# Moved small loads, an undrained block end and a last pair by column halves in an encoder layer

## The reference

```python
h = x + token_mixer(rms_norm(x, g_attn_norm), w_in, ..., w_out)
y = h + hier_moe(rms_norm(h, g_ffn_norm), ...)

def token_mixer(a, ...):
    c_q, c_kv, k_r, u = split(a @ w_in)            # 384, 256, 64, 512 columns
    q = (rms_norm(c_q) @ w_uq)                     # 4 heads of 192, RMS-norm per head, rotary on 64
    kv = (rms_norm(c_kv) @ w_ukv)                  # 4 heads of 128 + 128
    attn = softmax(q k^T / sqrt(192)) v            # both directions
    return concat([attn, multi_scale_pool(u)]) @ w_out

def hier_moe(x, ...):                              # 4 groups of 8 experts, top group, top 2 in it
    for e in range(32):
        hdn = silu(x @ w_gate[e]) * (x @ w_up[e])  # 1024 -> 256
        y = y + combine[:, e:e + 1] * (hdn @ w_down[e])
```

## Time and profile before

| | us |
|---|---|
| median of 3 runs (647.74 to 649.58) | 649.23 |
| the profiled execution | 643.12 |
| its span, first to last instruction | 641.5 |
| TensorE busy | 537.6 (84%) |
| VectorE busy | 216.9 (34%) |
| ScalarE busy | 168.7 (26%) |
| GpSimd busy | 137.8 (21%) |
| DMA | 140.69 MB, mean 219 GB/s |

### The profile page before, as it was taken

One profiled execution on the slowest core, in us unless ns is written; L12 is line 12 of the kernel. 1 busy time (PEld: TensorE's weight loads), 2 busy tenths in 40 slices (PEclk: granted clock), 3 DMA queues, 4 the chain that ended last, 5 costly groups with the idle time before them and its releaser, 6 DMA issues.

```text
span 641.5 us, 9145 instructions
## 1 busy us (share of the span) xinstructions
PE 537.6 (84%) x3140; PEld 380.6 (59%) x3141; DVE 216.9 (34%) x646; ACT 168.7 (26%) x412; POOL 137.8 (21%) x214
## 2 busy tenths in 40 slices
PE   3979999999898889899962989999878995778861
PEld 2859888887344477788852546665546653444540
DVE  2663342351768662445573111121111111111110
ACT  3563434332464521222331201121111111111100
POOL 6022321321154100011114002321201321101110
PEclk9989999999899999999985989999999999988887
DMA  8920000000432009433359979999999999999961
GB/s 202 379 104 22 13 34 1 0 1 1 170 100 65 1 33 372 180 130 112 100 188 370 351 230 393 382 370 379 381 368 415 393 382 360 375 379 389 395 233 20
DMA packets 28589, 140.69 MB, mean 219 GB/s; under 512 B 6339, under 2 KB 7078, under 8 KB 16246
## 3 DMA queue, kind: packets, MB, share of 16 engines
q1 hardware_dynamic: 20496, 122.89, 49.1%
q0 software_dynamic: 6288, 14.04, 9.2%
q10 hardware_dynamic: 1766, 3.25, 1.7%
HBM read 131.15 MB, written 16.46 MB: 230 GB/s over the span
## 4 chain that ended last, share of the span: by engine, by line
DMA 44%; PE 42%; DVE 6%; SPq 2%; issue 2%; ACT 2%; POOL 1%; POOLq 0%
DMA expert_w<-in_w_down 20%; DMA expert_w<-in_w_up 18%; PE ps L450 8%; PE ps L451 7%; PE ps L455 7%; DMA w_uq_raw<-in_w_uq 3%; PE ps L615 3%; PE ps L556 3%; PE ps L779 2%; PE ps L570 2%; DMA x_res<-in_x_prompt 2%; DMA g_rows<-token_rows,idx_all 1%; PE ps L795 1%; PE ps L573 1%; SPq L369 1%
## 5 line engine op out<-in xcount | busy, mean ns | idle before, releaser
L779 PE MATMUL ps<-expert_w,xT 128*64 128x256 f32 x1152 | 131.2, 384 | 19.7 <-DMA expert_w<-in_w_up 8.3
L779 PEld LDWEIGHTS ps<-expert_w,xT 128*64 128x64 f32 x1152 | 96.8, 138 | 58.0 <-issue 29.4
L795 PE MATMUL ps<-expert_w,hT 128*64 128x512 f32 x288 | 73.9, 659 | 18.7 <-DMA expert_w<-in_w_down 13.2
L1544 POOL DMA_INDIRECT out<-y_sb,idx_now x18 | 28.7, 1596 | 190.2 <-issue 142.2
L1387 DVE SCALAR_TENSOR_TENSOR hid<-s_act,gate,ps 128x256 f32<-128x256 f32 x18 | 12.0, 667 | 144.4 <-ACT s_act L1025 144.4
L795 PEld LDWEIGHTS ps<-expert_w,hT 128*64 128x64 f32 x288 | 24.9, 150 | 56.1 <-issue 56.1
L1025 ACT ACTIVATE s_act<-ps,gate 128x256 f32<-128x256 f32 x18 | 8.5, 473 | 134.3 <-PE ps L779 134.3
L450 PE MATMUL ps<-w_in_hi,aT_hi 128*128 128x384 f32 (+2 forms) x120 | 43.7, 369 | 0.0
L1399 DVE COPY y_sb<-ps 128x512 f32<-128x512 f32 x18 | 12.4, 692 | 86.3 <-PE ps L795 86.3
L451 PE MATMUL ps<-w_in_lo,aT_hi 128*128 128x384 f32 (+2 forms) x120 | 40.9, 345 | 0.0
L1030 ACT ACTIVATE y_sb<-ps 128x512 f32<-128x512 f32 x18 | 10.7, 597 | 89.6 <-PE ps L795 89.6
(11 more groups left out here) (235 smaller groups left out, 927.7 us busy)
## 6 DMA issues: line engine op xcount, KB each, us to landing
expert_w<-in_w_gate SPq DMA_DIRECT2D x32, 1024.0 KB, 9.5
expert_w<-in_w_up SPq DMA_DIRECT2D x32, 1024.0 KB, 9.1
expert_w<-in_w_down SPq DMA_DIRECT2D x32, 1024.0 KB, 9.8
w_in_raw<-in_w_in SPq DMA_DIRECT2D x8, 608.0 KB, 19.3
w_out_raw<-in_w_out SPq DMA_DIRECT2D x8, 512.0 KB, 3.8
out<-h_sb SPq DMA_DIRECT2D x6, 512.0 KB, 4.6
token_rows<-h_sb ACTq DMA_DIRECT2D x6, 512.0 KB, 4.9
x_sb<-in_x_prompt SPq DMA_DIRECT2D x4, 512.0 KB, 10.5
```

The lines of the kernel that those rows point to most:

```text
L779: mm = pe.matmul(ps[r, 2, g * FH:(g + 1) * FH], xT[:, q.o, k, r], w_gu(b, lane, k, g), start=(k == 0), stop=(k == KD - 1))
L795: mm = pe.matmul(ps[r, 4 + half, :], hT[:, q.o, k, r], w_dn(b, lane, k, half), start=(k == 0), stop=(k == 1))
L1544: pool.indirect_dma_start(out=out, out_offset=bass.IndirectOffsetOnAxis(ap=idx, axis=0), in_=y_sb[:, buf, :], in_offset=None, compute_op=A ...
```

## The change

Three edits in one.

1. The 14 DMAs at the head of GpSimd's list are issued by SP. The rotary table and the six broadcast gains stand behind w_ukv, ahead of the third x tile; the token numbers, routers, FFN gains, slot table and zeros (`small_tables`) stand behind the fourth x tile. VectorE multiplies the router's weights in token tile 4 instead of tile 1.
2. The block is opened with `no_gpsimd_drain=True`.
3. In the last pair w_down is loaded as four DMAs, column half by column half (`load_last_down`; the first two wait for `part_in[1]`, the others for `part_in[2]`, as the two of before did), TensorE waits for each half's load and signals after each half (`down_halves`), ScalarE copies the left half after the first signal, VectorE the right half after the second, and GpSimd adds each half by itself (`add_half`), with `out` seen as 1,536 rows of 512 columns and indices `idx_last` = 2 x token + half, which four small VectorE operations make ahead of the first pair. The second add doesn't wait for the first.

```diff
-        block = ctx.enter_context(nc.Block())
+        block = ctx.enter_context(nc.Block(no_gpsimd_drain=True))
...
             sp.dma_start(w_ukv[:, :, :], a["w_ukv"][0].rearrange("(k p) n -> p k n", k=KKV)).then_inc(w_ukv_in, 16)
+            small = [(rope_tab[:, :, :, :].rearrange("p n t r -> p (n t r)"), a["rope"])]
+            half = DR // 2
+            for n, name in enumerate(("g_q_head", "g_k_head")):
+                g = a[name][0:1, DN:DQK]
+                small += [(g_rope[:, 2 * n, :], g.partition_broadcast(P)),
+                          (g_rope[:, 2 * n + 1, 0:half], g[:, half:DR].partition_broadcast(P)),
+                          (g_rope[:, 2 * n + 1, half:DR], g[:, 0:half].partition_broadcast(P))]
+            with nc.allow_non_contiguous_dma(reason="a few hundred short rows"):
+                for dst, src in small:
+                    sp.dma_start(dst, src).then_inc(gains_in, 16)
...
                 load_x(i)
+                if i == 3:
+                    small_tables()
...
+            def load_last_down(j, b):
+                src = a["w_down"][0].rearrange("(l j) (p k) (n f) -> j n p l k f", l=2, k=2, n=2)
+                for n in range(2):
+                    sp.wait_ge(part_in[1 + n], 16 * (j + 1))
+                    for lane in range(2):
+                        dst = weights[b][:, lane, 2, :].rearrange("p (k n f) -> p n k f", k=2, n=2)
+                        sp.dma_start(dst[:, n], src[j, n, :, lane]).then_inc(part_in[4 + n], 16)
...
+            def down_halves(b, n):
+                pe.wait_ge(main.hT_done, n + 1)
+                for half in range(2):
+                    pe.wait_ge(part_in[4 + half], 16 * (n + 2))
+                    for k in range(2):
+                        for lane in range(2):
+                            r = slice(lane * LANE, (lane + 1) * LANE)
+                            mm = pe.matmul(ps[r, 4 + half, :], hT[:, 0, k, r], w_dn(b, lane, k, half),
+                                           start=(k == 0), stop=(k == 1))
+                    mm.then_inc(main.y_mm, 1)
...
-                if i == 1:
+                if i == 4:
                     dve.wait_ge(router_in, 16 * N_ROUTER)
...
+            for lane in range(2):
+                r = slice(lane * LANE, (lane + 1) * LANE)
+                last_slots = ps[r, 5, PAIRS * (lane + 1) - 1:PAIRS * (lane + 1)]
+                for n in range(2):
+                    dve.tensor_scalar(idx_last[r, n:n + 1], last_slots, 2.0, 2.0 * NO_TOKEN + n, ALU.mult, ALU.add).then_inc(idx_done, 1)
...
+            def add_half(n, buf):
+                c = slice(n * 512, (n + 1) * 512)
+                pool.indirect_dma_start(out=out.rearrange("t (n f) -> (t n) f", n=2),
+                                        out_offset=bass.IndirectOffsetOnAxis(ap=idx_last[:, n:n + 1], axis=0),
+                                        in_=y_sb[:, buf, c], in_offset=None, compute_op=ALU.add,
+                                        bounds_check=2 * T - 1, oob_is_err=False).then_inc(main.added, 16)
...
+                if last:
+                    ready((idx_done, 13), (main.y_act, j + 1), (main.added, 16 * j))
+                    add_half(0, b)
+                    ready((main.y_dve, j + 1))
+                    add_half(1, b)
...
-            pool.wait_ge(main.added, 16 * PAIRS)
+            pool.wait_ge(main.added, 16 * (PAIRS + 1))
```

More of the change, by code:

```diff
@@ L364, in load_x, with small_tables @@
                 sp.dma_start(x_sb[:, i % 2, :], x_dram(i)).then_inc(x_in[i % 2], 16)
+            def small_tables():
+                with nc.allow_non_contiguous_dma(reason="short rows"):
+                    for dst, src in ((tok_ids[:, :], a["tokens"]),
+                                     (w_router[:, :, 0:EG], a["w_group_router"][0].rearrange("(k p) n -> p k n", k=KD)),
+                                     (w_router[:, :, EG:], a["w_expert_router"][0].rearrange("(k p) n -> p k n", k=KD)),
+                                     (g_router[:, :], a["g_ffn_norm"][0].rearrange("(k p) -> p k", k=KD)),
+                                     (g_x[:, :], a["g_ffn_norm"][0].rearrange("(p k) -> p k", k=KD))):
+                        sp.dma_start(dst, src).then_inc(router_in, 16)
+                sp.dma_start(slot_table.rearrange("(a b) c -> a (b c)", a=P),
+                               a["slots"].rearrange("(a b) c -> a (b c)", a=P)).then_inc(setup_dram, 16)
+                sp.dma_start(out[T:T + P, :], a["zeros"]).then_inc(setup_dram, 16)
             load_x(0)
@@ L425, in refill @@
                 used(lambda q: q.y_mm)
-                load_pair(sp, j, b, range(4, 6))
+                if isinstance(j, int):
+                    load_last_down(j, b)
+                else:
+                    load_pair(sp, j, b, range(4, 6))
             with sp.Fori(1, PAIRS // 3) as i:
@@ L807, in pair @@
                 hidden_transposes(main, j)
-                for n in range(4, 6):
-                    pe.wait_ge(part_in[n], 16 * (j + 1))
-                pe_y_free(pe, j)
-                down(main, b, j)
+                if last:
+                    pe_y_free(pe, j)
+                    down_halves(b, j)
+                else:
+                    for n in range(4, 6):
+                        pe.wait_ge(part_in[n], 16 * (j + 1))
+                    pe_y_free(pe, j)
+                    down(main, b, j)
                 def again(n, p):
@@ L1394, in hT_copy, with y_copy @@
                 dve.tensor_copy(hT[:, q.o, :, :], ps[:, 3, 0:FH].rearrange("p (k t) -> p k t", k=2)).then_inc(q.hT_done, 1)
-            def y_copy(q, n, buf):
-                dve.wait_ge(q.y_mm, n + 1)
+            def y_copy(q, n, buf, last=False):
+                dve.wait_ge(q.y_mm, n + 2 if last else n + 1)
                 y_free(dve, q, n)
@@ L1409, in pair @@
                 hT_copy(main, j)
-                y_copy(main, j, b)
+                y_copy(main, j, b, last)
                 def again(n, p):
@@ L1573, in more_add @@
             def more_add(j, n):
-                ready((over.y_act, n + 1), (over.y_dve, n + 1), (main.added, 16 * (j + 1)))
+                halves = 1 if isinstance(j, int) and j == PAIRS - 1 else 0
+                ready((over.y_act, n + 1), (over.y_dve, n + 1), (main.added, 16 * (j + 1 + halves)))
                 add_rows(over, n, 3, idx_now[:, 6:7])
@@ L1588, in pair @@
                     gather_pair(j + 2, (b + 2) % 3, 2 * j + 1)
-                set_idx(3 + b, j)
-                waits = [(idx_set, add_count(j)), (main.y_act, j + 1), (main.y_dve, j + 1)]
-                if not (isinstance(j, int) and j == 0):
-                    waits.append((main.added, 16 * j))
-                ready(*waits)
-                add_rows(main, j, b, idx_now[:, 3 + b:4 + b])
+                if not last:
+                    set_idx(3 + b, j)
+                if last:
+                    ready((idx_done, 13), (main.y_act, j + 1), (main.added, 16 * j))
+                    add_half(0, b)
+                    ready((main.y_dve, j + 1))
+                    add_half(1, b)
+                else:
+                    waits = [(idx_set, add_count(j)), (main.y_act, j + 1), (main.y_dve, j + 1)]
+                    if not (isinstance(j, int) and j == 0):
+                        waits.append((main.added, 16 * j))
+                    ready(*waits)
+                    add_rows(main, j, b, idx_now[:, 3 + b:4 + b])
                 todo = pool.value_load(counts_i[0:1, 3, bass.ds(j, 1)], min_val=0, max_val=PASSES - 1)
```

30 lines of the change are left out of this document (5 added, 25 removed).

## The result

| | before | after |
|---|---|---|
| executions, us | 649.23, 649.58, 647.74, 649.05 | 624.22, 624.80, 629.76, 624.97 |
| median, us | 649.14 | 624.88 |
| profiled execution, us (its span) | 643.12 (641.5) | 624.22 (622.6) |

The ratio is 0.9646, 95% interval 0.9595 to 0.9697: the changed kernel takes 19.7 to 26.3 us less, 24.3 us by the medians. From the one profiled execution to the other it is 18.9 us, and there the forecast was 19.2.

A forecast was written before the change was run, and what follows sets the result against it. Bound: w_uq's late load for the first 35 us, then mostly TensorE to 340 us, expert weights from 377. Head 10.4 (9.1 + 1.3), drain 5.2 and tail 3.6 sum to 19.2 us off 649.23: 630.0, range 627 to 637.

The forecast's parts named there:

- the last step: Sum at the end: 10.4 + 5.2 + 3.6 = 19.2 us, subtracted from the timed median 649.23, gives 630.0.
- the tail: Last pair by column halves: matmuls start at hT's end, last landing at 631.9 against 635.5; 3.6 us, between 1.8 and 5.5.
- the head by w_uq: Start of the kernel: w_uq lands earlier, line 873 starts between 25.2 and 26.1 instead of 34.9; 9.1 us gained.
- the clock in tile 0: First token tile: TensorE hardly stands, so eight matmuls escape the low clock; 1.3 us, or 0.
- the drain: Closing barrier: GpSimd's 5.22 us drain goes with nothing beside it, so 5.2 us count in full.
- the issuer alone: Small loads: if the part changed only the issuer, it would give nothing by the skill's rule; time 640.4.
- Rope tables: Line 1122: table and six broadcasts land at 28 us at 15 ns a short row, 33 us being free.
- rival (b): Head held by something else, rope tables at the q0 price or slow early w_in rows: about 4 us remain, 636.4; chance 0.10.
- Other small loads: Seven loads behind the fourth x tile: 5 us, delaying at most the fifth tile, which has 28.7 us of slack.
- Rival (d): Short rows clog SP's in-order queue, the fifth x tile is late, slower than before: 651; chance 0.03.
- Rival (a): End of program: the drain's time comes back behind the block, profiled time minus span growing to 7 us: 635.2; chance 0.16.
- Rival (c): Last pair: halves give nothing, two short-row adds taking as long as one and weights landing late: 633.6; chance 0.08.

The follow-up runs named there:

- a2_after_look: The changed kernel, not altered, profiled a second time: 620.74 us.
- g1: The changed kernel with the 14 small loads issued by GpSimd, but late (seven once w_ukv has landed, seven in token tile 2): 629.12 us, ratio 0.9709.
- h1: The kernel before with only the small loads moved to SP behind the weights; drain and last pair as before: 635.11 us, ratio 0.9798.
- s1: The changed kernel with all 14 small loads issued by SP ahead of the weights, right behind the constants: 637.48 us, ratio 0.982.
- b1: An exact copy of the kernel before, timed and profiled again: 649.94 us, ratio 1.001.
- b2: An exact copy of the kernel before, run for another profile: 646.0 us.
- b4: An exact copy of the kernel before, run for another profile: 645.46 us.
- b3: An exact copy of the kernel before, run for another profile: 647.93 us.
- d1: The kernel before with only the GpSimd drain at the end of the block removed: 643.5 us, ratio 0.9915.
- t1: The kernel before with only the last pair's down loads, matmuls, copies and row-adds done by halves: 641.24 us, ratio 0.9888.
- n1: The changed kernel with the small loads back on GpSimd at the start; no drain and the last pair by halves stay: 639.67 us, ratio 0.9869.

## Why the prediction was right and wrong

**The step that failed** is the size of the gain that the last step took off the median: "The median of the timed runs is 649.23, 6.1 above the profiled one; I subtract from the median: 630.0". What was taken off was 10.4 + 5.2 + 3.6 = 19.2 us; the stages show 22.7 in the mean and the medians 24.3. Every term was short: the tail 3.6 against 5.1, the head by w_uq 9.1 against 10.1, the clock in tile 0 1.3 against 2.0, the drain 5.2 against 5.5. They were read from one execution that had a short head, a short attention and a short tail, and taken off the median of executions in which most of these were longer; and the range was built only from the bounds of the prices. A gain read in a short head and a short tail is too small for the usual ones. Of the 5.1 us between 630.0 and 624.88, 1.7 are terms that were short even from profile to profile, 1.8 more are the difference between that profile and the mean, and 1.6 no run places.

The 18.9 measured between the two profiled executions against 19.2 looks like a hit, and so does 624.22 against 623.9, and it is partly chance: the attention of the changed kernel's profiled execution was a long one, which hid 2.2 us of the gain. Had I written that the two executions may differ by 2 to 3 us in stages that the change doesn't touch, the range would have reached down by that much, to the result.

**Term by term**, with the means of the stage table (eight profiles with the old head, seven with the old tail; five with the new head, a2_after_look among them, four of these for the tile loop, since g1's late tables lengthen it; five with the new tail; the end of h1, whose drain was short, left out):

| term | predicted | profile to profile | mean of stages |
|---|---|---|---|
| w_uq, line 873 | 9.1 (8.8 to 9.7) | 9.4 | 10.1 |
| clock in tile 0 | 1.3 (0 to 1.3) | 1.4 | 2.0 |
| no drain | 5.2 (5.2 to 5.3) | 5.6 | 5.5 |
| tail | 3.6 (1.8 to 5.5) | 4.5 | 5.1 |
| sum | 19.2 | 20.9 | 22.7 |

Profile to profile the other stages take back 2.0 us of the 20.9. Of the 24.3 us between the medians the means explain 22.7; the rest is less than the interval's half width of 3.3. Each term lies above the middle that I took, three of them above the end that I had for them, none by more than 0.7 us. The misses have one sign, in part because three of them share a source, the short head, low stretch and tail of the profile of before; but from profile to profile the tail is already 0.9 short and the head 0.3. The end's 0.3 to 0.4 us is the handshake of the barrier behind the drain, which shrank too (before: 635.5 to 641.5 with 5.22 of drain; after: 622.2 to 622.6).

**Head: right, mechanism and place.** q0 is gone, the rows come 1.5 us apart, w_uq is scaled at 25.5 (forecast: before 26.2), line 873 starts at 25.41 (25.2 to 26.1). I took the later of two landings, 23.5; it was 22.88. TensorE and ScalarE end together, at 25.1 and 25.5, as worked out. That it is the order and not the issuer is shown in the head by the two runs on it (40.0 and 26.75 us), as the prediction had it. What I priced there, 640.4 for the issuer alone, came out as 637.5, but not by nothing changing: its head is 3.2 us longer than the mean before, its tile loop 2.0 shorter, and the rest of the difference is open.

**Clock in tile 0: right, and larger.** In a stretch of 5 us from about the first c transposes on the eight profiles with the old head show a granted clock of 0.50 to 0.78, behind a stand of 2.4 to 3.1 us, the changed kernel 1.00 behind one of 0.98, and s1, where TensorE stands 1.07 us ahead of them, loses nothing either. The profile that I read had a short low stretch, 3.4 us; it and the three others with one (b1, b2, b4) have a tile loop of 123.2 to 123.4 us. In b3, d1, t1 and n1 it lasts 6.8 us, the clock is 0.50 or 0.57, as here in d1:

```profile
37.80:42.80 5.00, 3.79 (x13) 0.50 0.02 5
```

and the loop takes 123.9 to 124.7. My 1.3 us were the price of the short one.

**Rope tables: wrong price, no loss.** I priced a broadcast row at 15 ns of an engine, from the bias loads. The six broadcasts landed at 25.6, 26.3, 27.3, 28.9, 31.35 and 33.9 us, 0.7 to 2.6 us apart, with the engines less than a third busy, and most of the bytes those of the x tiles behind them:

```profile
q1 hardware_dynamic: 1167, 0.81, 31.7%
```

(the DMA view of the changed kernel, 25.6 to 33.9 us). Ahead of everything, in s1, they landed 1.1 to 1.4 us apart. From 7 to 10 us the queue had nothing else there, and the engines were 9% busy:

```profile
q1 hardware_dynamic: 357, 0.05, 8.7%
```

So the price is one of time per load and not of engine time: in these loads 128 rows that all read one short piece of DRAM take 1 us or more, behind one another. It is no rule for all such loads: the two bias broadcasts of the kernel before landed 0.3 us each behind the load ahead of them (240.96, 241.25 and 241.52 us). Why is open. The old queue's price didn't fit either: in the trace of before the six broadcasts went over q0 as 96 packets of 1,024 and 2,048 bytes, not as 768 rows. The prediction had a wait at line 1122 among the signs of being wrong. So the cause that rival (b) names was there by half: the tables came 5.9 us later than by my price and 5 us sooner than by the q0 price, 39. Its effect was not: VectorE had room until somewhere between 33.9 and 37.1 us. With the tables at 37.1 the run on the order gave 629.1.

**Other small loads: right.** They landed between 35 and 42 us, and the fifth x tile is asked for at 51.3. Rival (d) needed 50 us for them.

**Drain: right.** Rival (a) is out: the profiled time minus the span is 1.6 us in before and in after. The Trainium skill, Runtime: NRT & Kernel Launch, The ~15µs preamble/postamble breakdown, lists a closing barrier of about 1.5 us, which would have left room for it; no run here shows time coming back.

**Tail: right in every step, each a little short.** The matmuls start 0.26 us behind hT, not 1.96. Gate and up to the start of VectorE's copy is 6.2 us (9.1 before): 2.9 gained where I had 2.5, since the clock is full from 609.6 to 616 us:

```profile
609.60:616.00 6.40, 4.18 (x18) 1.25 (x18) 1.29 (x3) 1.07 (x2) 0.57 (x1) 1.00 0.39 143
```

I had left half 0 at the low level or the full one, 622.3 or 624.0, and taken something between. From the copy to the landing it is 6.4 us (8.0 before), 1.6 gained where I had 1.1; from the end of the issue to the landing 3.3, estimated at 3.6. The last landing follows the last w_down by 8.4 us, forecast 9.5, before 13.1. Rival (c) is out. The old tail ran at a granted clock of 0.66 to 0.82 in all five profiles of the kernel before, so its slow matmuls were usual, and in four of the five the low stretch was longer (6.8 us) than in the one I read (3.4).

## What to carry to other kernels

Loads that nobody needs yet belong behind those that somebody waits for, in the same queue or by a wait in another: it is the order that gains, and one looks next at what the moved loads themselves must be in time for, and by how much. A gain read from one profiled execution is to be set against that execution; if it lies well off the median, one asks in which stages, and the range takes in what untouched stages do from one execution to the next. A closing instruction of 5 us at the end of one engine is worth the same as 5 us of matmuls, and is found in the chain's last rows, not among the busy groups.

## What the runs showed of the hardware that I had not expected

- Broadcast loads of the head gains, 128 short rows from one place in DRAM each, landed 0.7 to 2.6 us apart on SP's queue in the changed kernel, 1.1 to 1.4 in s1 with the engines 9% busy; on GpSimd's queue 1.0 to 1.7 in the kernel before, 0.5 to 2.1 over all eight profiles with the old head. For these six it is the number of loads that counts, not their 16 to 32 KB; the two bias broadcasts took 0.3 us each.
- SP's own issue of one load takes from 0.33 us to several: 5.43 us for the FFN gains in the router's layout in s1, 4.28 for the token numbers in the changed kernel, both behind many short rows, but also 6.45 for w_ukv in the kernel before, behind long ones and beside GpSimd's loads. Short rows are not the only thing that holds it up.
- GpSimd's drain at the block's end took 5.22 us in the five profiles of the kernel before, 4.08 in h1 and 5.30 in t1, with all its DMAs landed; without it the time around the span stayed at 1.6 to 1.8 us.
- In the last pair TensorE's granted clock fell in all seven profiles in which it stood 2.1 to 2.5 us for the last w_down (0.66 to 0.81), and in none of the seven with the products in halves.
- The attention stage of one and the same program takes 72.4 to 75.0 us, and its length goes with the place of TensorE's low stretch (8 us behind the first scores: 72.4; 22 us: 74.7 to 75.0).
- The low stretch behind the stand of 3 us lasted 3.4 or 6.8 us, from one execution of a program to the next.
